# Differential attention mixed before the product, and the HGRN output norm moved to GpSimd

## The chip, the cores and the metric

One core of one Trainium2 chip runs the whole program. The metric is the device time of one launch in microseconds; 0.3% of it is 7.1 us.

## The reference, cut to what matters

The program is two transformer blocks on 512 tokens of width 1024, in float32. The change touches the mixer of the first layer only. Its two halves are a differential attention (4 heads, two score matrices of head width 64 each, values of width 128) and an HGRN2 recurrence (4 heads of width 128), both normed by an RMS norm over the 128 channels of a head:

```
s  = einsum('bhcqd,bhckd->bhcqk', q, k)          # c = 0, 1; causal mask
pr = softmax(s, axis=-1)
a  = pr[:, :, 0] - lam * pr[:, :, 1]
o_a = rms_norm(einsum('bhqk,bhkd->bhqd', a, v), sub_g) * (1 - lam_init)
o_b = rms_norm(hgrn_output, hg_g) * gate          # gate * hg_g is HG in the kernel
mix = concat([o_a, o_b]) @ w_out
```

## The kernel before, in words

Each engine has its own instruction list, written out by hand; they meet at counted semaphores. All large products run as three float32r products (high times high, high times low, low times high): ScalarE casts each 128x1024 weight piece to `w_h` (L803), VectorE makes the remainder `w_l` (L1300), TensorE multiplies (L2202).

The differential attention is a loop over 16 steps (4 heads, and in each head 4 tiles of 128 queries, with 128, 256, 384 and 512 keys, so each head is a period of 4 steps), called `diff_steps`. In its loop every engine handles several steps at once. At loop index k:

- TensorE: scores of step k for both c (`scores`, L2283), after VectorE's maxima of step k-2; transposes of both probability matrices of step k-2 (`trans`, L2292); products with the values of step k-3, one for each c (`values`, L2307). At k = 3 `keep_busy` (L2276) multiplies a weight piece 16 times into a bank that nobody reads. A float32 product is two instructions in the trace, a transpose is one.
- ScalarE: copies the transposed probabilities of step k-2 out of two PSUM banks in one instruction (`copy_pt`, L850), then the two exponentials of step k with their row sums (L841).
- VectorE: masks and takes the maxima of step k (`row_max`, L1436, in place for both c), then finishes step k-3 (`output` and `difference`): reciprocals of the row sums (L1446), times minus lambda (L1504), the two products scaled and added out of PSUM (L1505, L1506), and the square sum for the norm (L1495).
- GpSimd only issues DMAs; its next one (L716) waits for the last step's output.

The HGRN norm is laid between: its root (L907) is taken on ScalarE before the loop, VectorE forms the reciprocal at k = 1 (L1796) and scales `HI` at k = 2 to 5 (four 128x128 instructions of L1801 each). TensorE transposes the four 128-channel chunks of `HI` at k = 8, 10, 12 and 14 (L2455), ScalarE copies them at k = 9, 11, 13 and 15, after the exponentials of that step (L1100), and VectorE takes the remainder behind it at the same k (L1807).

After the loop `tail` begins: TensorE waits for the last output of the attention, multiplies two pieces of the output matrix with the HGRN half (L2202), then transposes the normed attention heads (L2244). Beside it ScalarE takes the root of the attention's norm (L907) and casts a piece, VectorE makes its remainder and norms 16 head tiles (L1818).

Of the kernel before, what the change touches and what calls it, by code (L numbers as in the profile page):

```python
# [24 lines left out]
P = 128  # L25
# [175 lines left out]
def bass_two_blocks(nc, t, consts, route_consts, tokens, slot_y, out):  # L201
    ctx = ExitStack()
    with ctx:
# [406 lines left out]
        OT_LAG = 4  # L610
        T_BANK, V_BANK, O_BANK = 4, 6, 7

        def row(v):

            return v.rearrange("(o n) -> o n", o=1).partition_broadcast(P) if len(v.shape) == 1 else v
# [98 lines left out]
        def _(pool):  # L714
            def load(dst, src_ap, name, **kw):
                pool.dma_start(dst, src_ap, **kw).then_inc(sem(name), 16)  # L716
# [15 lines left out]
            def tail(layer, mixer):  # L732
# [9 lines left out]
                load(GAIN[1], row(t["ln2_b"][layer]), "gain_a")  # L742

# [47 lines left out]
        def _(act):  # L791
# [310 lines left out]
            attention("diff", diff_steps, d_probs, d_pt, extra=hgrn_chunk)  # L1102
            root("sub", sd[:, 16:32], ms[:, 16:32], 1.0 / P, eps1)
# [182 lines left out]
        def _(dve):  # L1286
# [216 lines left out]
            def difference(k, w, inv):  # L1503
                own.mark(V.tensor_tensor(inv[:, 1:2], inv[:, 1:2], nlam, ALU.mult))  # L1504
                own.do(V.tensor_scalar(w.out, bank[V_BANK][:, 0:P], inv[:, 0:1], None, ALU.mult))  # L1505
                V.scalar_tensor_tensor(w.out, bank[V_BANK][:, P:2 * P], inv[:, 1:2], w.out, ALU.mult, ALU.add)\  # L1506
                    .then_inc(sem("at_out"), 1)
                dve.wait_ge(sem("at_out"), un.start["diff"] + k + 1)
                square_sum(w.out, 16 + 4 * (k % NT) + k // NT)
# [283 lines left out]
            def hgrn_norm(k):  # L1793
                if k == 1:
                    dve.wait_ge(sem("hg.root"), 1)
                    own.do(V.reciprocal(rs[:, 0:16], sd[:, 0:16]))  # L1796
                if 2 <= k < 6:
                    i = k - 2
                    for h in range(4):
                        hv = slice(h * P, (h + 1) * P)  # L1800
                        ins = V.scalar_tensor_tensor(HI[:, i, hv], HI[:, i, hv], rs[:, 4 * i + h:4 * i + h + 1],  # L1801
                                                     HG[:, i, hv], ALU.mult, ALU.mult)
                    ins.then_inc(sem("src_ready"), 1)
# [6 lines left out]
            attention("diff", diff_steps, d_probs, difference, extra=hgrn_norm)  # L1810
            tell(sem("sub.stat"))
# [347 lines left out]
        def _(pe):  # L2159
# [298 lines left out]
            attention("diff", diff_steps, d_probs, d_pt, warm=tail0[0][0], extra=hgrn_transposed)  # L2458
# [214 lines left out]
```

## Time and profile before

| | |
|---|---|
| median of 3 runs | 2375.17 us (2369.21 to 2375.31) |
| the profiled execution | 2371.46 us, its span 2369.6 us |
| TensorE busy, of the span | 94% |
| VectorE, ScalarE, GpSimd busy | 55%, 47%, 2% |
| the differential attention loop | about 210 to 265 us of the span |
| TensorE's granted clock, mean | 0.979 |

The span is that of the one core. Busy times of TensorE overlap a little, since its matmuls are pipelined; starts are exact, so distances between starts are what to read.

### The profile page before, as it was taken

How to read it: one execution, taken by the hardware profiler on the slowest of the kernel's cores; microseconds unless marked ns; L12 is line 12 of the kernel's file. 1: busy time of each engine (PE TensorE's matmuls, PEld its weight loads, DVE VectorE, ACT ScalarE, POOL GpSimd, SP SyncE). 2: the span in 40 equal slices, each digit the busy share in tenths (PEclk: the TensorE clock that was granted, in tenths of full speed). 3: DMA queues.
4: the chain of work that ended last, by engine and by line, in shares of the span. 5: the costliest groups of instructions: out<-in, count | busy, mean ns of one | idle time of the engine just before them, and what ended most of it. 6: DMA issues, size and time to landing. Idle time of an engine off the chain costs nothing.

```text
span 2369.6 us, 30065 instructions
## 1 busy us (share of the span) xinstructions
PE 2230.6 (94%) x11002; PEld 1819.0 (77%) x11002; DVE 1302.7 (55%) x1916; ACT 1107.1 (47%) x1646; POOL 54.8 (2%) x70
## 2 busy tenths in 40 slices
PE   6999999999999999999999999799999769999994
PEld 5877788888888776788888877568888558888883
DVE  3456663333374436553333467542454469998995
ACT  3435453433432237262442353363234358888884
POOL 1000000000000000000000000000000010000001
PEclk8999999999999999999999999899999979999997
DMA  5221233223322220233323232203223189999995
GB/s 166 94 71 36 74 105 103 93 96 98 98 89 89 80 72 1 89 125 98 97 91 104 80 107 93 63 28 97 90 72 98 58 332 403 410 410 408 409 401 186
DMA packets 129138, 338.59 MB, mean 143 GB/s; under 512 B 10528, under 2 KB 11712, under 8 KB 129040
## 3 DMA queue, kind: packets, MB, share of 16 engines
q1 hardware_dynamic: 117744, 296.85, 35.5%
q0 software_dynamic: 7840, 27.59, 3.4%
q10 hardware_dynamic: 3456, 12.81, 1.3%
q8 instruction: 65, 1.06, 0.2%
q14 instruction: 33, 0.27, 0.0%
HBM read 320.96 MB, written 16.25 MB: 142 GB/s over the span
## 4 chain that ended last, share of the span: by engine, by line
PE 86%; DVE 8%; ACT 4%; DMA 1%; issue 1%; SPq 0%; POOL 0%; DVEq 0%; ACTq 0%; POOLq 0%
PE bank L2202 40%; PE bank L2205 18%; PE bank L2582 10%; PE bank L2619 5%; PE bank L2283 2%; PE bank L2292 2%; PE bank L2353 1%; PE bank L2226 1%; DVE w_l L1300 1%; PE bank L2562 1%; PE bank L2307 1%; DMA w_raw<-in_ev_w_in_dram 1%; ACT w_h L803 1%; DVE stat L1332 1%; DVE xt_l L1367 1%
## 5 line engine op out<-in xcount | busy, mean ns | idle before, releaser
L1300 DVE TENSOR_TENSOR w_l<-w_raw,w_h 128x1024 fp32r<-128x1024 f32 x370 | 447.8, 1222 | 615.2 <-ACT w_h L803 612.1
L803 ACT CAST w_h<-w_raw 128x1024 fp32r<-128x1024 f32 x370 | 385.6, 1051 | 748.3 <-PE bank L2202 521.6
L2202 PE MATMUL bank<-w_h,xt_h 128*128 128x512 f32 (+1 forms) x960 | 377.2, 393 | 18.2 <-DVE w_l L1300 7.5
L2202 PE MATMUL bank<-w_h,xt_l 128*128 128x512 f32 (+1 forms) x960 | 372.5, 388 | 0.0
L2202 PE MATMUL bank<-w_l,xt_h 128*128 128x512 f32 (+1 forms) x960 | 372.4, 388 | 0.0
L2205 PE MATMUL bank<-xt_h,w_h 128*128 128x512 f32 x608 | 237.5, 391 | 12.0 <-DVE xt_l L1322 9.6
L2202 PE MATMUL bank<-w_h,ht_h 128*128 128x512 f32 x624 | 244.0, 391 | 0.7 <-DVE w_l L1300 0.7
L1300 DVE TENSOR_TENSOR w_l<-spare,w_h 128x1024 fp32r<-128x1024 f32 x184 | 220.6, 1220 | 41.5 <-ACT w_h L803 41.1
L2202 PE MATMUL bank<-w_h,ht_l 128*128 128x512 f32 x624 | 242.9, 389 | 0.0
L2202 PE MATMUL bank<-w_l,ht_h 128*128 128x512 f32 x624 | 242.8, 389 | 0.0
L2205 PE MATMUL bank<-xt_h,w_l 128*128 128x512 f32 x608 | 237.3, 390 | 0.0
L2205 PE MATMUL bank<-xt_l,w_h 128*128 128x512 f32 x608 | 237.1, 390 | 0.0
L2202 PEld LDWEIGHTS bank<-w_h,xt_h 128*128 128x128 f32 x960 | 181.4, 189 | 58.4 <-issue 12.0
L803 ACT CAST w_h<-spare 128x1024 fp32r<-128x1024 f32 x184 | 193.7, 1053 | 49.9 <-PE bank L2619 22.9
L2202 PEld LDWEIGHTS bank<-w_h,xt_l 128*128 128x128 f32 x960 | 181.5, 189 | 37.3
L2202 PEld LDWEIGHTS bank<-w_l,xt_h 128*128 128x128 f32 x960 | 181.7, 189 | 35.1
L2582 PE MATMUL bank<-w_h,xt_h 128*128 128x512 f32 x368 | 148.9, 405 | 2.4 <-DVE xt_l L2104 2.4
L2582 PE MATMUL bank<-w_h,xt_l 128*128 128x512 f32 x368 | 145.0, 394 | 0.0
L2582 PE MATMUL bank<-w_l,xt_h 128*128 128x512 f32 x368 | 144.1, 391 | 0.0
L2205 PEld LDWEIGHTS bank<-xt_h,w_h 128*128 128x128 f32 x608 | 114.6, 188 | 36.8 <-issue 13.0
L2202 PEld LDWEIGHTS bank<-w_h,ht_h 128*128 128x128 f32 x624 | 117.1, 188 | 25.5 <-DVE w_l L1300 1.5
L2202 PEld LDWEIGHTS bank<-w_h,ht_l 128*128 128x128 f32 x624 | 117.1, 188 | 24.3
(355 smaller groups left out, 2926.3 us busy)
## 6 DMA issues: line engine op xcount, KB each, us to landing
w_raw<-in_ffn_w_dram SPq DMA_DIRECT2D x128, 512.0 KB, 3.7
spare<-in_w_down_dram SPq DMA_DIRECT2D x92, 512.0 KB, 6.9
spare<-in_w_gate_dram SPq DMA_DIRECT2D x88, 512.0 KB, 7.2
w_raw<-in_w_up_dram SPq DMA_DIRECT2D x88, 512.0 KB, 6.6
w_raw<-in_w_in_dram SPq DMA_DIRECT2D x30, 512.0 KB, 3.8
w_raw<-in_ev_w_in_dram SPq DMA_DIRECT2D x28, 512.0 KB, 3.6
w_raw<-in_od_w_in_dram SPq DMA_DIRECT2D x24, 512.0 KB, 3.7
slot_y_dram<-slot_out ACTq DMA_DIRECT2D x23, 512.0 KB, 6.8
```

The lines of the kernel that those rows point to most:

```text
L803: nc.scalar.copy(w_h[:, n % SLOTS, :], raw_of(n)).then_inc(sem("w_hi"), 1)
L1300: V.tensor_tensor(w_l[:, s_, :], raw_of(n), w_h[:, s_, :].bitcast(F32), ALU.subtract)\
L1332: own.mark(V.bn_stats(bn[:, i, a, :], src_v[:, i, a * HALF:(a + 1) * HALF]))
L1367: V.tensor_tensor(xt_l[:, chunks, toks_of(i)], tile_bank(name, i, half).rearrange("p (c s) -> p c s", c=4), xt_h[:, chunks, toks_of(i)].bi ...
L2202: mm = T.matmul(bank[set0 + m][:, 0:g.width], a[:, c, toks_of(m)], b[:, kk, :], start=first, stop=last)
L2205: mm = T.matmul(bank[set0 + m][:, 0:g.toks], b[:, kk, m * P:(m + 1) * P], a[:, c, 0:g.toks], start=first, stop=last)
L2226: mm = T.transpose(tile_bank(name, i, half)[:, toks_of(c)], src_tile(i, 4 * half + c), ident)
L2283: T.matmul(bank[2 * (k % 2) + c][:, 0:w.keys], q, key, start=True, stop=True)\
L2292: mm = T.transpose(bank[T_BANK + c][:, toks_of(b)], probs[:, k % 3, c, toks_of(b)], ident)
L2307: mm = T.matmul(bank[V_BANK][:, c * w.dv:(c + 1) * w.dv], pt[:, k % 2, c, toks_of(b)], v, start=b == 0, stop=b == len(w.values[c]) - 1)
L2582: mm = T.matmul(bank[g.bank[0]][:, :], a, b[:, kk, :], start=j == kk == p == 0, stop=j == 3 and kk == 1 and p == 2)
L2619: mm = T.matmul(bank[g.bank[half]][:, :], a[:, j, :], b, start=j == p == 0, stop=j == 3 and p == 2)
```

## The change

`OUTPUT` is 3. The two probability matrices of a step are scaled by their reciprocal sums (the second also by minus lambda) and added on VectorE right after the exponentials. One matrix per step is then transposed, copied and multiplied. The output of a step leaves PSUM by a plain copy on VectorE; its square sum moves to ScalarE. The scaling of the HGRN output moves to GpSimd, as 16 scalings of `HG` and 4 multiplications into `HI`, which start when VectorE has the reciprocals at k = 1. The transposes alternate between two PSUM banks. The new TensorE loop has no `keep_busy`. The attention's root now waits for ScalarE's own squares.

```diff
@@ GpSimd, before tail(0, "dilated")
+            pool.wait_ge(sem("hg.scale"), 1)
+            for i in range(NT):
+                for h in range(4):
+                    hv = slice(h * P, (h + 1) * P)
+                    nc.gpsimd.tensor_scalar(HG[:, i, hv], HG[:, i, hv], rs[:, 4 * i + h:4 * i + h + 1], None, ALU.mult)                        .then_inc(sem("hg.scaled"), 1)
+            for i in range(NT):
+                pool.wait_ge(sem("hg.scaled"), 4 * i + 4)
+                nc.gpsimd.tensor_tensor(HI[:, i, :], HI[:, i, :], HG[:, i, :], ALU.mult).then_inc(sem("src_ready"), 1)
@@ ScalarE
-            attention("diff", diff_steps, d_probs, d_pt, extra=hgrn_chunk)
-            root("sub", sd[:, 16:32], ms[:, 16:32], 1.0 / P, eps1)
+                for k in range(n + OUTPUT):
+                    if k >= OUTPUT:
+                        u = k - OUTPUT
+                        col = 16 + 4 * (u % NT) + u // NT
+                        act.wait_ge(sem("at_out"), u + 1)
+                        nc.scalar.activation(spare[...], diff_steps[u].out,
+                                             ACT.Square, accum_out=ms[:, col:col + 1]).then_inc(sem("at_square"), 1)
+                    if TRANS <= k < n + TRANS:
+                        t_, w = k - TRANS, diff_steps[k - TRANS]
+                        act.wait_ge(sem("at_trans"), t_ + 1)
+                        if t_ >= 2:
+                            act.wait_ge(sem("at_values"), t_ - 1)
+                        nc.scalar.copy(d_pt[:, t_ % 2, 0, 0:w.keys], bank[T_BANK + t_ % 2][:, 0:w.keys])\
+                            .then_inc(sem("at_ptcopy"), 1)
+                    if k < n:
+                        for c in range(2):
+                            p = d_probs[:, k % 3, c, 0:diff_steps[k].keys]
+                            act.wait_ge(sem("at_max"), 2 * k + c + 1)
+                            nc.scalar.activation(p, p, ACT.Exp, scale=-1.0, bias=neg_max[:, k % 4, c:c + 1],
+                                                 accum_out=row_sum[:, k % 4, c:c + 1]).then_inc(sem("at_prob"), 1)
+                    hgrn_chunk(k)
+            act.wait_ge(sem("at_square"), len(diff_steps))
+            nc.scalar.activation(sd[:, 16:32], ms[:, 16:32], ACT.Sqrt, bias=eps1, scale=1.0 / P)
@@ VectorE
+                for k in range(n + OUTPUT):
+                    if k < n:
+                        row_max(0, k, diff_steps[k], d_probs)
+                    if k >= OUTPUT:
+                        u = k - OUTPUT
+                        dve.wait_ge(sem("at_values"), u + 1)
+                        V.tensor_copy(diff_steps[u].out, bank[V_BANK][:, 0:P]).then_inc(sem("at_out"), 1)
+                    if 1 <= k <= n:
+                        c = k - 1
+                        p0, p1 = (d_probs[:, c % 3, b, 0:diff_steps[c].keys] for b in range(2))
+                        inv = inv_sum[:, c % 2, :]
+                        dve.wait_ge(sem("at_prob"), 2 * c + 2)
+                        own.do(V.reciprocal(inv, row_sum[:, c % 4, :]))
+                        own.do(V.tensor_scalar(p1, p1, inv[:, 1:2], nlam, ALU.mult, ALU.mult))
+                        V.scalar_tensor_tensor(p0, p0, inv[:, 0:1], p1, ALU.mult, ALU.add).then_inc(sem("at_mixed"), 1)
+                    hgrn_norm(k)
@@ TensorE
+                for k in range(n + OUTPUT):
+                    if k < n:
+                        scores(0, k, diff_steps[k])
+                    if k >= OUTPUT:
+                        u, w = k - OUTPUT, diff_steps[k - OUTPUT]
+                        pe.wait_ge(sem("at_ptcopy"), u + 1)
+                        if u:
+                            pe.wait_ge(sem("at_out"), u)
...
+                    if TRANS <= k < n + TRANS:
+                        t_ = k - TRANS
+                        pe.wait_ge(sem("at_mixed"), t_ + 1)
...
+                    hgrn_transposed(k)
```

## Rows read from the trace of the kernel before

**Rows 1.** The page's first part: busy time, share of the span, instructions.

```profile
PE 2230.6 (94%) x11002; PEld 1819.0 (77%) x11002; DVE 1302.7 (55%) x1916; ACT 1107.1 (47%) x1646; POOL 54.8 (2%) x70
```

**Rows 2.** Busy time in a stretch: from:to, length, engines, granted clock, DMA.

```profile
220.00:230.00 10.00, 9.80 (x69) 7.14 (x70) 9.60 (x46) 6.91 (x20) 0.00 (x0) 1.00 0.01 2
```

**Rows 3.** Chain of waits, in order of time: start, length, what.

```profile
215.25 3.85 PE bank L2276 x16
...
224.09 1.05 DVE arena L1801 x4
...
264.92 8.46 PE bank L2202 x36
273.38 1.43 PE bank L2244 x13
```

**Rows 4.** TensorE's timeline: start, length, line, count, idle before with its releaser.

```profile
210.05 2.00 PE L2283 MATMUL bank<-arena 64*128 64x128 f32 x12 [1.06 <-ACT arena L824]
...
247.01 1.09 PE L2292 MATMUL bank<-cst,arena 128*128 128x128 f32 x8
...
250.63 2.02 PE L2307 MATMUL bank<-spare,arena 128*128 128x128 f32 x16
```

**Rows 5.** VectorE's timeline.

```profile
210.57 0.29 DVE L1436 CUSTOM_DVE_ANT_0 arena<-bank,cst 128x128 f32<-128x128 f32 x1 [7.02 <-PE bank L2283]
...
215.39 0.69 DVE L1436 CUSTOM_DVE_ANT_0 arena<-bank,cst 128x512 f32<-128x512 f32 x1 [1.31 <-PE bank L2283]
...
216.62 0.08 DVE L1436 DVE_READ_ACCUMULATOR2_ANT small<- 128x1 f32 x1
...
229.01 0.16 DVE L1446 RECIPROCAL small<-small 128x2 f32<-128x2 f32 x1
...
230.26 0.69 DVE L1436 CUSTOM_DVE_ANT_0 arena<-bank,cst 128x512 f32<-128x512 f32 x1
...
250.74 0.69 DVE L1807 TENSOR_TENSOR xt_l<-bank,xt_h 128x512 fp32r<-128x512 f32 x1
...
267.99 4.29 DVE L1818 SCALAR_TENSOR_TENSOR arena<-arena,stat,small 128x128 f32<-128x128 f32 x16
```

**Rows 6.** ScalarE's timeline.

```profile
212.93 0.40 ACT L841 ACTIVATE arena<-arena,small 128x128 f32<-128x128 f32 x1
...
213.71 0.49 ACT L841 ACTIVATE arena<-arena,small 128x256 f32<-128x256 f32 x1
...
219.57 0.58 ACT L850 COPY arena<-bank 128x512 f32<-128x512 f32 x1 [3.32 <-PE bank L2292]
220.06 0.72 ACT L841 ACTIVATE arena<-arena,small 128x512 f32<-128x512 f32 x1
...
221.48 0.78 ACT L850 COPY arena<-bank 128x768 f32<-128x768 f32 x1
...
260.16 1.28 ACT L907 ACT_TABLE_LOAD   x1
```

**Rows 7.** VectorE's groups by line and shape: count, busy, mean ns, idle before.

```profile
L1516 DVE SCALAR_TENSOR_TENSOR arena<-X,bank 128x512 f32<-128x512 f32 x16 | 10.8, 685 | 9.5 <-PE bank L2202 9.5
L1505 DVE TENSOR_SCALAR arena<-bank,small 128x128 f32<-128x128 f32 x16 | 5.5, 344 | 0.0
L1687 DVE TENSOR_SCALAR arena<-arena,small 128x512 f32<-128x512 f32 x4 | 2.2, 544 | 0.1
```

**Rows 8.** GpSimd's only 128x512 computation, of its groups by line.

```profile
L718 POOL MEMSET arena<- 128x512 f32 x1 | 0.5, 524 | 0.3 <-POOLq L2653 0.3
```

**Rows 9.** Busy time around two loops' ends: the second ("dilated") and this one.

```profile
946.00:956.00 10.00, 6.22 (x65) 4.47 (x63) 5.01 (x11) 5.68 (x10) 1.20 (x2) 1.00 0.01 2
...
958.00:962.00 4.00, 4.00 (x14) 3.14 (x12) 0.00 (x0) 0.00 (x0) 0.00 (x0) 0.64 0.99 286
966.00:970.00 4.00, 4.00 (x20) 3.30 (x19) 0.07 (x1) 1.05 (x1) 0.00 (x0) 1.00 0.43 131
...
251.00:264.00 13.00, 10.81 (x81) 8.80 (x80) 8.28 (x35) 6.83 (x14) 0.00 (x0) 1.00 0.01 1
```

More of the change, by code:

```diff
@@ L610, in bass_two_blocks @@
         OT_LAG = 4
+        OUTPUT = 3
         T_BANK, V_BANK, O_BANK = 4, 6, 7
@@ L1501, in scaled, with differences @@
                                 inv.unsqueeze(2).to_broadcast([P, 2, w.dv]), ALU.mult).then_inc(sem("at_out"), 1)
[L1503 to L1509, printed above, removed]
+            def differences():
+                n = len(diff_steps)
+                for k in range(n + OUTPUT):
[14 more added lines that the diff above has]
+                    hgrn_norm(k)
             def tail(layer, groups):
@@ L1795, in hgrn_norm @@
                     dve.wait_ge(sem("hg.root"), 1)
[L1796 to L1803, printed above, removed]
+                    V.reciprocal(rs[:, 0:16], sd[:, 0:16]).then_inc(sem("hg.scale"), 1)
                 if k in (9, 11, 13, 15):
@@ L1808, in hgrn_norm @@
                         .then_inc(sem("tr_lo"), 1)
-            attention("diff", diff_steps, d_probs, difference, extra=hgrn_norm)
-            tell(sem("sub.stat"))
+            differences()
             split(tail0[0][0].n + LOOK, None, 0)
@@ L2456, in hgrn_transposed, with differences @@
                     mm.then_inc(sem("tr_done"), 1)
-            attention("diff", diff_steps, d_probs, d_pt, warm=tail0[0][0], extra=hgrn_transposed)
+            def differences():
+                n = len(diff_steps)
+                for k in range(n + OUTPUT):
[6 more added lines that the diff above has]
+                            pe.wait_ge(sem("at_out"), u)
+                        for b, v in enumerate(w.values[0]):
+                            mm = T.matmul(bank[V_BANK][:, 0:P], d_pt[:, u % 2, 0, toks_of(b)], v,
+                                          start=b == 0, stop=b == len(w.values[0]) - 1)
+                        mm.then_inc(sem("at_values"), 1)
+                    if TRANS <= k < n + TRANS:
+                        t_ = k - TRANS
+                        pe.wait_ge(sem("at_mixed"), t_ + 1)
+                        if t_ >= 2:
+                            pe.wait_ge(sem("at_ptcopy"), t_ - 1)
+                        for b in range(diff_steps[t_].keys // P):
+                            mm = T.transpose(bank[T_BANK + t_ % 2][:, toks_of(b)], d_probs[:, t_ % 3, 0, toks_of(b)],
+                                             ident)
+                        mm.then_inc(sem("at_trans"), 1)
+                    hgrn_transposed(k)
+                pe.wait_ge(sem("at_out"), n)
+            differences()
             tail(0, tail0)
```

6 lines of the change are left out of this document (added).

## The prediction

> **What bounds the kernel now.** TensorE is busy 94% of the span [rows 1], so only a stretch where it waits, or does work that can go, is worth anything. The change touches one such stretch, 210 to 265 us. In the stretch table TensorE (9.8 of 10 us) and VectorE (9.6) are both full [rows 2]; ScalarE is not. The chain of waits says what set the pace: the 16 idle multiplications of L2276 (3.85 us), then VectorE with the HGRN scalings (1.05 us for four, in four steps), later TensorE [rows 3]. The loop ends at 264.87, TensorE's product begins at 264.92 [rows 3]. All that the change can win is how much earlier that product begins; call the loop's end T. The whole loop lasts 54 us, so even 10% of it is 0.23% of the kernel.
>
> **TensorE, removed.** Of each step's transposes and value products half go. The 8 transposes of a 512-key step take 1.09 us, the 16 instructions of its products 2.02 [rows 4]; a head has 20 and 40 of these, so 2.7 and 5.0 us, and half is 3.9 us per head, 15 over four. L2276's 3.85 us go too. TensorE is left with about 3 us of scores, 1.4 of transposes, 2.5 of products, in two heads 0.9 for HGRN: some 7 to 8 us per head, where a head took 12. It is no longer the bound.
>
> **VectorE, removed and added.** The finish of a step took 229.01 to 230.26, 1.25 us [rows 5], 20 us in all, and the 16 HGRN scalings 4.3 [rows 3]; both go. Added are, per step, a 128x128 copy out of PSUM and the mixing. The copy: the nearest rows are a 0.29 us instruction that is followed 0.21 later by the next, and L1505 with 0.34 [rows 5, 7]; I take 0.21, as nothing waits for its end on VectorE. Mixing: a reciprocal, 0.19 with its wait [rows 5]; the scaling, whose nearest rows are 0.344 at 128 columns and 0.544 at 512 [rows 7], so 0.34, 0.41, 0.48, 0.54 plus 0.03 for the wait; the two-input instruction, 0.27 at 128 (1.05 for four of L1801 [rows 3]) and 0.65 at 512 (0.685 less the overlap [rows 7]). Sums for 128, 256, 384, 512 keys: 0.83, 1.03, 1.23, 1.41, so 4.5 per head. Bounds: the scaling at the two-input rate (0.69 at 512) adds 0.3 per head; at half its rate (0.27) it takes 0.5 off. The maxima stay: 2 x (0.29 - 0.08) = 0.43 at 128 keys, 1.22 at 512 [rows 5], 0.70 and 0.96 between, 3.3 per head. VectorE now has 3.3 + 0.85 + 4.5 = 8.65 us per head without HGRN work, and it is the bound.
>
> **The new waits.** ScalarE gets a square per step at the head of its loop index, waiting for VectorE's copy of step k-3, which stands behind the maxima of step k. So from the end of the maxima of step k ScalarE needs 0.34 (copy, signals), 0.39 (square, by the 0.39 pace of a 128-column exponential with its sum), the copy of one matrix (0.17 to 0.49 [rows 6]) and the exponentials of step k: 0.78 at 128 keys, 1.42 at 512 [rows 6], 0.98 and 1.22 between. VectorE meanwhile does copy, mixing of k-1 and the maxima of k+1, then needs those exponentials. Most steps fit; the mixing of a 512-key step comes 0.37 too early, and the product of step 3 delays k = 6 by 0.4. At k = 9 and 13 VectorE also waits for ScalarE's HGRN copy, queued behind the exponentials: 0.34 + 0.39 + 0.49 + 0.98 + 0.57 + 0.05 = 2.82, then its own 0.60 (0.69 less the overlap [rows 5]), so 3.42 after the maxima, where copy and mixing alone take 1.04. At k = 11 and 15: 0.34 + 0.39 + 0.25 + 1.42 + 0.57 + 0.05 + 0.60 = 3.62. Behind the waiting VectorE stand the next maxima, and all engines wait for these.
>
> **Sum, clock kept.** Maxima of step 0 at 210.57 as before. The first mixing needs the exponentials of step 0, done at 213.8 (212.93 plus two [rows 6]): mixed at 214.7, the HGRN reciprocal at 214.95, then 215.9 (maxima 2), 216.95, 218.15 and 218.35 (maxima 3, copy), 219.6 (mixing 2). k = 4: 0.43 + 0.21 + a wait for the exponentials of step 3 + 1.41, to 222.0; k = 5 1.75, k = 6 2.6, k = 7 2.66, to 229.0. k = 8 2.42, k = 9 4.12, k = 10 2.2, k = 11 4.84, to 242.6. k = 12 2.05 (no wait, ScalarE is ahead), k = 13 4.12, k = 14 2.2, k = 15 4.84, to 255.8. Then copy and mixing 15: 257.45; four transposes 0.65, copy 0.6, four products 1.13 with signals, copy 0.3: T = 260.4. Before it was 264.87: 4.5 us are won, of the 20 and more that TensorE lost in work. Of these, 6.7 us stand as VectorE's four waits for ScalarE (1.78, 1.58, 1.78, 1.58).
>
> **After T.** The root's table load (1.28 us) stood in the idle time before [rows 6]; now squares come last and it falls between the last square and the root. Square 0.5, load, root 0.3, cast and remainder of a piece 2.2, reciprocal 0.3, four scalings per tile: the four tiles are ready at T + 5.7 to T + 8.9, against T + 7.4 before (267.99 + 4.29 [rows 5]). TensorE reaches their transposes at T + 8.46 [rows 3] and the last tile's a microsecond later, so this costs nothing; without that cover of two pieces it would cost 1.5 us.
>
> **GpSimd.** It starts at about 215.0, and TensorE needs `HI` at k = 8, after the transposes of step 6, at about 229.3. So 20 instructions have 14.3 us, 0.71 each. The only row is a 128x512 memset of 0.524 [rows 8], where VectorE's two-input 128x512 takes 0.69 [rows 7]. Lower end, VectorE's speed: 16 x 0.35 + 4 x 0.69 = 8.4 us. Upper end, three times that: 25 us. I take something near 11, hidden. The Trainium skill, "GPSIMD Engine Reference", section "Engine selection", calls GpSimd about 2x slower on two inputs and about line rate on one: an estimate of 16 x 0.35 + 4 x 1.38 = 11 us, in time; no row here shows it. Its section "Key points" says that GpSimd shares SBUF interfaces with VectorE, which speaks against the change: both could be slowed from 215 to 226, where five mixings (5.5 us) stand.
>
> **The clock.** The other loop's end is the row to weigh: TensorE busy 6.2 of 10 us, then idle 2.3 us, and the granted clock fell (0.64 in 958 to 962, 14 matmuls in 4 us where 20 fit later [rows 9]); that is 6 x 0.2 = 1.2 us there and 1.6 with what lies ahead of it. This loop's end kept 1.00 with 10.8 of 13 [rows 9]. After the change TensorE does about 3.5 us of work in the last 9 (251 to 260), with a gap of over 2 us while the last mixing waits: I expect a fall to 1.2 GHz and charge 1.6. At the start TensorE is idle from 212.05 [rows 4] to 214.7 and does some 2.5 us of work up to 219.5, with no L2276 to fill it; a fall there is half hidden behind VectorE: 0.5. Together 2.1 us; bounds 0 and 5.
>
> **The forecast.** -4.5 + 2.1 = -2.4 us: 2371.5 becomes 2369.1 for an execution like the profiled one. That one stood 3.7 us below the median shown; against the median 2375.2 it is 2372.8.
>
> **Rivals.**
> 1. ScalarE's queue doesn't hold VectorE back at k = 9 to 15 (its squares or copies are shorter): the waits of 1.78, 1.58, 1.78, 1.58 go, 6.7 us, and with the clock's loss the change is -9, 2366. For: ScalarE has only about 8.3 us of work per head. Against: before, too, L1807 waited 0.43 us twice. 10%.
> 2. The clock stays at 1.00: -4.5, 2370.7. For: no fall here before. Against: rows 9. 20%.
> 3. The clock falls again and again, as TensorE has under 60% of work from k = 9 on: each fall costs up to 1.7 us, four of them 7; less 4.5, +2.5 to +5, 2379. Against: a slow TensorE is a busy one, 7.5 us of work become 14 per head. 12%.
> 4. Slower: GpSimd is late. At three times VectorE's times its 25 us end at 240; TensorE holds its k = 8 transposes, and with them scores 9, for 10 us, and all follow one for one: +8, 2383. It decides from 0.71 us mean per instruction, and turns the sign at about 0.85. The skill's shared interface would act here. 10%.
> 5. The forecast's own case, 2369 to 2375.5: 48%.
>
> **How the numbers follow.** What this measurement can tell is about 0.3%, 7 us. Faster than that needs rival 1 or a run of cheap terms: 0.12. Slower needs rival 4 or a bad 3: 0.16. The rest is 0.72. The range from 2365 to 2380 leaves out rival 4 and the far end of 1; unknown terms are mixing (-2 to +1.3), clock (0 to +5), and the median's own 4 us.
>
> **What would show it.** Right: the value products L2307 gone, their successors at half the count; L1807's instruction idle 1.5 to 1.8 us for ScalarE four times; VectorE's maxima of step 8 at about 229; TensorE's first product of the tail near 260.4; granted clock under 1 in the 4 us behind it; GpSimd done before 229. Wrong: TensorE waiting for GpSimd at step 8, a scaling at 0.3 us per 512 columns or over 0.7, or a product of the tail waiting for the normed heads.

## The result, and the profile after

The changed kernel takes 2375.7 us (median of 20 runs, 2373.5 to 2380.3) where the kernel before takes 2370.9 (20 runs beside it, 2367.3 to 2376.6): a ratio of 1.0017, 95% interval 1.0010 to 1.0025. By the ratio it is 4 us slower (the medians lie 4.8 apart), where 2.4 us of gain were forecast. The profiled execution has a span of 2371.8 us, before 2369.6.

The page's first part, which answers to [rows 1]: TensorE lost 6.8 us of busy time and 136 instructions, and the time did not follow. About 20 us less work was forecast for TensorE; a part of its remaining work ran at half the clock and so counts for more busy time.

```profile
PE 2223.8 (94%) x10866; PEld 1809.7 (76%) x10866; DVE 1304.0 (55%) x1868; ACT 1107.6 (47%) x1678; POOL 69.8 (3%) x90
```

The stretch table from the first scores to the first product of the tail (I call this the loop), and the 12 us behind it: first the kernel after, then the kernel before, whose loop ran from TensorE's 210.05 [rows 4] to 264.92 [rows 3].

```profile
208.60:268.23 59.63, 42.63 (x200) 27.83 (x200) 41.13 (x133) 33.83 (x118) 15.37 (x20) 0.76 0.00 1
268.23:280.23 12.00, 12.00 (x57) 10.12 (x58) 7.39 (x20) 5.17 (x9) 2.44 (x4) 0.92 0.74 236
```
```profile
210.05:264.92 54.87, 49.20 (x337) 36.96 (x337) 39.37 (x180) 34.80 (x88) 0.00 (x0) 1.00 0.00 1
264.92:276.92 12.00, 12.00 (x61) 10.19 (x62) 8.55 (x24) 4.35 (x7) 2.36 (x4) 1.00 0.77 257
```

The loop became 4.76 us longer, at a mean granted clock of 0.76 in place of 1.00, and the tail's first pieces lost 0.9 us more: from the first product to the heads' transposes TensorE took 9.19 us (to 277.42), before 8.30 (to 273.22; the 8.46 of [rows 3] is a busy time that overlaps them). The spans differ by less: this loop happened to start 1.45 us earlier, and behind the other loop the clock fell before (0.64 [rows 9]) and not after (1.00 in all of 956 to 970), which is 1.6 us by the prediction's reckoning. The loops of the kernels below start anywhere from 208.13 to 211.62 us, though nothing ahead of them was changed, so I compare loops and ratios, not spans.

VectorE's timeline around step 5's mixing, then GpSimd's. The columns are start, length, what, and in brackets the idle time before with its releaser.

```profile
214.50 0.45 DVE L1555 TENSOR_SCALAR arena<-arena,small 128x256 f32<-128x256 f32 x1
...
217.51 0.62 DVE L1556 SCALAR_TENSOR_TENSOR arena<-arena,small 128x384 f32<-128x384 f32 x1
...
225.16 3.94 DVE L1555 TENSOR_SCALAR arena<-arena,small 128x256 f32<-128x256 f32 x1
229.15 0.48 DVE L1556 SCALAR_TENSOR_TENSOR arena<-arena,small 128x256 f32<-128x256 f32 x1
229.55 0.68 DVE L1472 CUSTOM_DVE_ANT_0 arena<-bank,cst 128x512 f32<-128x512 f32 x1
```
```profile
213.59 10.46 POOL L749 TENSOR_SCALAR arena<-arena,stat 128x128 f32<-128x128 f32 x16 [206.68 <-DVE stat L1844]
224.03 4.93 POOL L752 TENSOR_TENSOR arena<-arena 128x512 f32<-128x512 f32 x4
```

A scaling of 128x256 that takes 0.45 us at 214.50 takes 3.94 at 225.16. It ends at 229.10, 0.14 after the last of GpSimd's four two-input products (224.03 + 4.93 = 228.96). During GpSimd's 16 scalings, which have one tensor input, VectorE ran at its usual pace.

TensorE's timeline:

```profile
217.63 1.22 PE L2509 MATMUL bank<-spare,arena 128*128 128x128 f32 x4 [0.70 <-ACT arena L1126]
...
229.68 0.69 PE L2518 MATMUL bank<-cst,arena 128*128 128x128 f32 x2 [3.37 <-DVE arena L1556]
231.80 1.22 PE L2509 MATMUL bank<-spare,arena 128*128 128x128 f32 x4 [0.70 <-ACT arena L1126]
...
244.50 0.71 PE L2509 MATMUL bank<-spare,arena 128*128 128x128 f32 x4 [1.26 <-ACT arena L1126]
...
262.60 1.65 PE L2509 MATMUL bank<-spare,arena 128*128 128x128 f32 x6 [2.46 <-ACT arena L1126]
...
265.78 2.07 PE L2509 MATMUL bank<-spare,arena 128*128 128x128 f32 x8 [0.67 <-ACT arena L1126]
268.23 0.80 PE L2242 MATMUL bank<-w_h,xt_h 128*128 128x512 f32 x1 [0.39 <-DVE arena L1548]
```

At 229.68 it had waited 3.37 us for the mixed matrix behind that scaling. The same four instructions take 1.22 us at one place and 0.71 at another: the clock. The stretch table in pieces of 4 us (the clock is the third number from the end; 0.50 is 1.2 GHz, 1.00 is 2.4) shows four falls, the last of them in the drain, by which I mean the steps after the last scores:

```profile
216.00:220.00 4.00, 3.30 (x14) 2.47 (x15) 3.51 (x16) 2.86 (x11) 4.00 (x7) 0.50 0.00 0
...
224.00:228.00 4.00, 2.31 (x14) 1.20 (x12) 3.96 (x7) 2.22 (x9) 4.00 (x5) 1.00 0.00 0
...
232.00:236.00 4.00, 4.00 (x17) 3.02 (x18) 2.57 (x10) 2.73 (x11) 0.00 (x0) 0.50 0.03 6
...
240.00:244.00 4.00, 3.03 (x16) 1.52 (x16) 3.89 (x16) 1.97 (x8) 0.00 (x0) 1.00 0.00 0
...
248.00:252.00 4.00, 4.00 (x18) 2.86 (x18) 2.79 (x10) 1.81 (x10) 0.00 (x0) 0.50 0.00 0
...
264.00:268.00 4.00, 3.17 (x14) 2.48 (x12) 0.41 (x2) 0.99 (x3) 0.00 (x0) 0.50 0.00 0
```

VectorE's four waits for ScalarE's HGRN copy, and its last copy:

```profile
239.45 0.69 DVE L1848 TENSOR_TENSOR xt_l<-bank,xt_h 128x512 fp32r<-128x512 f32 x1 [1.55 <-ACT xt_h L1110]
...
246.37 0.69 DVE L1848 TENSOR_TENSOR xt_l<-bank,xt_h 128x512 fp32r<-128x512 f32 x1 [1.37 <-ACT xt_h L1110]
...
253.94 0.69 DVE L1848 TENSOR_TENSOR xt_l<-bank,xt_h 128x512 fp32r<-128x512 f32 x1 [1.79 <-ACT xt_h L1110]
...
260.86 0.69 DVE L1848 TENSOR_TENSOR xt_l<-bank,xt_h 128x512 fp32r<-128x512 f32 x1 [1.37 <-ACT xt_h L1110]
...
267.89 0.29 DVE L1548 COPY arena<-bank 128x128 f32<-128x128 f32 x1 [3.31 <-PE bank L2509]
```

### The profile page after: what moved, and what is told of

Read it like the earlier page. It is cut to its first block, busy times and chain, and to the rows that moved or that the text cites. A ratio compares the mean times of both kernels' runs of the same rounds, so it can differ in the third digit from the quotient of the medians.

```text
span 2371.8 us, 29784 instructions
## 1 busy us (share of the span) xinstructions
PE 2223.8 (94%) x10866; PEld 1809.7 (76%) x10866; DVE 1304.0 (55%) x1868; ACT 1107.6 (47%) x1678; POOL 69.8 (3%) x90
## 3 DMA queue, kind: packets, MB, share of 16 engines
q8 instruction: 63, 1.03, 0.2%
## 4 chain that ended last, share of the span: by engine, by line
PE 85%; DVE 8%; ACT 4%; issue 1%; DMA 1%; POOL 0%; SPq 0%; ACTq 0%; DVEq 0%; POOLq 0%
PE bank L2242 40%; PE bank L2245 18%; PE bank L2648 10%; PE bank L2685 5%; PE bank L2323 2%; PE bank L2332 2%; PE bank L2393 1%; DVE w_l L1336 1%; PE bank L2266 1%; PE bank L2628 1%; ACT w_h L813 1%; DMA X<-in_x_dram 1%; DVE stat L1368 1%; DVE xt_l L1403 1%; ACT arena L834 1%
```

## The experiments

The theories: A, GpSimd's norm blocks VectorE; B, the clock falls because TensorE has too little to do; C, ScalarE's order (the square ahead of a step's exponentials, HGRN's copy behind them) holds VectorE. The recorded expectations call them Theory 2, Theory 1 and Theory 3; those of d1_chunk and d2_square use the letters A to C for other things. All ran beside the kernel before. "Loop" is as above, from each one's profiled execution; the kernel before has 54.87 us at clock 1.00, the changed one 59.63 at 0.76. There is one trace of each kernel, and it need not be a typical execution: that of a7_pieces is the shortest of five (2374.7, median 2378.8), that of a5_order the longest of seven (2368.8, median 2365.5), that of d2_square 3.3 us under its median.

| kernel | loop, us | clock | median / beside it before, us | ratio [95%] |
|---|---|---|---|---|
| a1_keep | 60.71 | 0.82 | 2376.4 / 2373.9 | 1.0025 [1.0010, 1.0040] |
| a2_norm | 57.06 | 0.78 | 2374.3 / 2373.9 | 1.0007 [0.9997, 1.0017] |
| a3_both | 59.27 | 0.85 | 2377.5 / 2373.9 | 1.0017 [1.0007, 1.0027] |
| b1_pool | 62.51 | 0.92 | 2376.9 / 2373.9 | 1.0013 [1.0004, 1.0021] |
| a7_pieces | 58.26 | 0.77 | 2378.8 / 2370.8 | 1.0035 [1.0022, 1.0049] |
| c4_one_input | 56.05 | 0.77 | 2374.5 / 2372.8 | 1.0012 [1.0002, 1.0022] |
| a4_fill | 56.19 | 0.97 | 2373.2 / 2370.8 | 1.0003 [0.9994, 1.0012] |
| a5_order | 51.30 | 0.97 | 2365.5 / 2370.8 | 0.9976 [0.9965, 0.9987] |
| a6_order | 51.09 | 0.80 | 2366.3 / 2370.8 | 0.9976 [0.9966, 0.9985] |
| c3_before_order | 56.02 | 0.97 | 2372.3 / 2372.8 | 0.9992 [0.9982, 1.0003] |
| d1_chunk | 51.35 | 0.84 | 2368.9 / 2372.0 | 0.9992 [0.9980, 1.0003] |
| d2_square | 54.49 | 0.78 | 2374.3 / 2372.0 | 1.0004 [0.9992, 1.0016] |
| c1_order_pool | 50.12 | 0.80 | 2366.4 / 2372.8 | 0.9975 [0.9966, 0.9985] |
| c2_split | 49.53 | 0.83 | 2365.7 / 2372.8 | 0.9979 [0.9970, 0.9989] |
| d3_split_fill | 46.93 | 0.96 | 2363.0 / 2372.0 | 0.9962 [0.9948, 0.9976] |

### Idle products back, and the norm back on VectorE

a1_keep, from the changed kernel, after the scores of k = 3:

```diff
+                    if k == 3:
+                        keep_busy(tail0[0][0], 16, O_BANK)
```

> The changed kernel with the 16 idle multiplications put back at k = 3. Theory 1 (the granted clock): in the changed kernel it fell to 1.2 GHz at 215.5, 229, 246.5 and 260; the filling ends the first fall only. It takes 3.9 us itself at full clock, most of it in front of VectorE's next maxima, so the loop stays at 59 to 61 us (59.6 without) and the kernel within 1.5 us of the changed one. Rival (the missing idle multiplications are what made the change lose): the clock stays at 1.00 through the loop, the loop gets 3 us or more shorter. Theory 2 (GpSimd blocks VectorE): the 3.9 us scaling of 256 columns stays in either case.

a2_norm, from the changed kernel (GpSimd's 20 instructions gone):

```diff
-                    V.reciprocal(rs[:, 0:16], sd[:, 0:16]).then_inc(sem("hg.scale"), 1)
+                    own.do(V.reciprocal(rs[:, 0:16], sd[:, 0:16]))
+                if 2 <= k < 6:
+                    i = k - 2
+                    for h in range(4):
+                        hv = slice(h * P, (h + 1) * P)
+                        ins = V.scalar_tensor_tensor(HI[:, i, hv], HI[:, i, hv], rs[:, 4 * i + h:4 * i + h + 1],
+                                                     HG[:, i, hv], ALU.mult, ALU.mult)
+                    ins.then_inc(sem("src_ready"), 1)
```

> The changed kernel with the HGRN norm back on VectorE (16 scalings at k = 2 to 5). Theory 2 (GpSimd's four two-input instructions, 224.0 to 229.0, hold a port that VectorE's scaling of probabilities needs): no such scaling takes over 0.6 us where one took 3.94; the 3.5 us are won, the scalings cost up to 4.3, and the clock's fall at 229 goes or moves: loop 57.5 to 60 us against 59.6, the kernel 0 to 2 us faster. Rival (the 3.94 us come from ScalarE or from TensorE and only show there): a scaling of 3 us or more stays, and the kernel is 4 us slower.

a3_both has both edits.

> Both at once: the norm on VectorE and the 16 idle multiplications at k = 3. Under theories 1 and 2 together no first fall of the clock, no blocked scaling; loop 58 to 61 us, since the HGRN scalings of VectorE fall beside the idle multiplications as before the change, and the kernel at the time of the one before (within 3 us). Rival (neither matters, it is ScalarE's queue alone): the loop stays at 59.6 plus what was put back, 62 or more.

TensorE of a1_keep, and VectorE's mixing of step 3 with the block in another place:

```profile
218.20 5.82 PE L2316 MATMUL bank<-w_h 128*128 128x512 f32 x16
```
```profile
224.28 0.29 DVE L1548 COPY arena<-bank 128x128 f32<-128x128 f32 x1 [4.55 <-PE bank L2511]
...
226.91 1.54 DVE L1555 TENSOR_SCALAR arena<-arena,small 128x512 f32<-128x512 f32 x1
228.49 1.63 DVE L1556 SCALAR_TENSOR_TENSOR arena<-arena,small 128x512 f32<-128x512 f32 x1
```

The idle products stand in front of work: the copy of step 0 waited 4.55 us behind them, and the loop grew by 1.1 us. They did not prevent the first fall either: the granted clock was 0.50 from 216 to 222, and the 16 took 5.82 us where they took 3.85 before [rows 3]. Of a1_keep's twelve executions seven took 2373.6 to 2376.9 us and five 2382.6 to 2386.1; the trace is of one of the seven, and what made the five longer is open.

The norm on VectorE takes 2.6 us off the loop though VectorE has 4.3 us more to do [rows 3]. That speaks for A, and 2.2 us over the kernel before stay. In the times it is not clear of the noise: 1.0007 [0.9997, 1.0017] against 1.0017 [1.0010, 1.0025]. Both edits together (a3_both) have a loop of 59.27, as expected, but did not come within 3 us of the kernel before: the idle products cost 2.2 us of loop over a2_norm, most of what the norm's move gave.

### The norm on GpSimd alone

b1_pool is the kernel before with only the GpSimd part: its 20 instructions in, VectorE's 16 out.

> The kernel before with only the HGRN norm moved to GpSimd. It has no VectorE instruction in this loop that reads and writes SBUF alone with one input, so under theory 2 nothing is blocked: VectorE loses 4.3 us of scalings in k = 2 to 5, on the path there, and the loop gets 1.5 to 4 us shorter (54.9 before); the kernel 1.5 to 4 us faster. Rival (GpSimd slows all of VectorE's SBUF work, or is late at k = 8): the maxima of 224 to 229 take longer than 0.7 us, or TensorE waits for GpSimd, and nothing is won.

VectorE, GpSimd and TensorE of b1_pool:

```profile
221.72 4.50 DVE L1514 TENSOR_TENSOR small<-small 128x1 f32<-128x1 f32 x1
...
229.29 0.16 DVE L1514 TENSOR_TENSOR small<-small 128x1 f32<-128x1 f32 x1
```
```profile
221.26 4.93 POOL L752 TENSOR_TENSOR arena<-arena 128x512 f32<-128x512 f32 x4
```
```profile
227.01 2.04 PE L2310 MATMUL bank<-spare,arena 128*128 128x128 f32 x8 [4.30 <-DVE arena L1516]
```

A multiplication of one element per partition, which takes 0.16 us elsewhere, took 4.50 and ended at 226.22 with GpSimd's products (226.19). The expectation of no block fell: a two-input instruction of VectorE is held as well, here one of 128x1. This half of the change, by itself, makes the loop 7.6 us longer in the profiled execution and costs 1.3 per mille of the time, 3 us. Not all of the 7.6 is the block. An early fall of the clock stands ahead of it, and c3_before_order (below), which has nothing on GpSimd, has it too; first b1_pool, then c3_before_order:

```profile
214.00:218.00 4.00, 4.00 (x11) 2.05 (x11) 1.31 (x4) 2.17 (x9) 4.00 (x8) 0.57 0.00 0
```
```profile
216.00:218.00 2.00, 2.00 (x5) 1.04 (x4) 1.02 (x3) 0.94 (x4) 0.00 (x0) 0.50 0.00 0
```

Counted from the first scores, VectorE's maxima of step 4 come 1.6 us later than in the kernel before in c3_before_order, and 5.9 us later in b1_pool: 1.6 of early fall and 4.3 of block. Another 1.6 us follow up to step 9, where the clock is down again (0.54 in 224 to 230). How often an execution has such a block and how long it is, one trace can't say.

### What of GpSimd's work blocks

a7_pieces cuts each of GpSimd's products into four:

```diff
-                nc.gpsimd.tensor_tensor(HI[:, i, :], HI[:, i, :], HG[:, i, :], ALU.mult).then_inc(sem("src_ready"), 1)
+                for h in range(4):
+                    hv = slice(h * P, (h + 1) * P)
+                    ins = nc.gpsimd.tensor_tensor(HI[:, i, hv], HI[:, i, hv], HG[:, i, hv], ALU.mult)
+                    ins.then_inc(sem("hg.product"), 1)
+            for i in range(NT):
+                pool.wait_ge(sem("hg.product"), 4 * i + 4)
+                pool.sem_inc(sem("src_ready"), 1)
```

> The changed kernel with GpSimd's four two-input multiplications of 128x512 cut into 16 of 128x128. Theory 2a (VectorE gets the port only between GpSimd's two-input instructions, and only when GpSimd lets go): with pieces of about 0.4 us VectorE's scaling waits at most 0.5 us at a time and its longest takes under 1.5 us, the loop 56 to 58 us. Theory 2b (a run of queued two-input instructions holds the port to its end): the scaling again takes 3 to 6 us, to the end of the last piece, and the loop is 59.6 or more.

c4_one_input gives them one tensor input; what it leaves out is the product of the HGRN output with its gate:

```diff
-                nc.gpsimd.tensor_tensor(HI[:, i, :], HI[:, i, :], HG[:, i, :], ALU.mult).then_inc(sem("src_ready"), 1)
+                nc.gpsimd.tensor_scalar(HI[:, i, :], HI[:, i, :], 1.0, None, ALU.mult).then_inc(sem("src_ready"), 1)
```

> The changed kernel with GpSimd's four 128x512 products of two inputs replaced by four 128x512 scalings by 1.0 of one input; what it leaves out is the product of the HGRN output with its gate. If two inputs are what takes the port: no VectorE scaling above 0.7 us, loop 55 to 57 us against 59.6. Rival (any GpSimd instruction of 512 columns holds the port): a VectorE instruction of 1.5 us or more stays in 224 to 229, the loop 58 to 60.

GpSimd of a7_pieces and VectorE's scaling of step 5 in it, then the same two of c4_one_input:

```profile
225.10 7.50 POOL L754 TENSOR_TENSOR arena<-arena 128x128 f32<-128x128 f32 x16
```
```profile
226.62 0.75 DVE L1561 TENSOR_SCALAR arena<-arena,small 128x256 f32<-128x256 f32 x1
```
```profile
225.71 5.98 POOL L752 TENSOR_SCALAR arena<-arena 128x512 f32<-128x512 f32 x4
```
```profile
226.66 0.68 DVE L1555 TENSOR_SCALAR arena<-arena,small 128x256 f32<-128x256 f32 x1
```

With one input GpSimd is busy longer (1.50 us per 128x512, where two inputs took 1.23), and VectorE loses at most 0.3 us on an instruction in place of 3.5, about 1 us over four instructions. The loop is 3.6 us shorter than with two inputs. So A is shown in the traces: what holds VectorE for long is GpSimd's 128x512 products of two tensor inputs, not its being busy. The price in time is not pinned: 1.0012 [1.0002, 1.0022] with one input, 1.0017 [1.0010, 1.0025] with two. In pieces of 128x128 the long block is gone too, with two inputs; but only 1.4 us of the loop are, and 0.7 of those are lost again behind it (9.92 us to the heads' transposes, 9.19 in the changed kernel). GpSimd's products last 7.50 us in place of 4.93. Its ratio, 1.0035, is the worst of all, which its trace, of the shortest of its five executions, does not explain; that stays open.

### The clock

a4_fill is a2_norm with idle 128x512 products (`filler`) ahead of TensorE's wait for each mixed matrix, 61 in all, and a wait for the weight piece that they read ahead of the loop (not shown):

```diff
-                        pe.wait_ge(sem("at_mixed"), t_ + 1)
                         if t_ >= 2:
                             pe.wait_ge(sem("at_ptcopy"), t_ - 1)
+                        filler(10 if t_ == 0 else 6 if k >= n else 3, T_BANK + t_ % 2)
+                        pe.wait_ge(sem("at_mixed"), t_ + 1)
```

> The changed kernel with the HGRN norm on VectorE and idle 128x512 multiplications before each wait for a mixed matrix: 10 at the first, 3 at each step, 6 at the last two. With the norm on VectorE alone the loop took 57.06 us and the granted clock was 0.78 in it. Theory 1 (the falls of the clock cost the time): the clock stays at 0.97 or more, TensorE's transposes and products take half, and the loop comes to 52 to 54.5 us; the product behind it runs at full clock, another 0.8 us. The kernel is 3 to 6 us faster than the changed one with the norm on VectorE. Rival (the clock is only a sign of idle time; VectorE and ScalarE set the pace): the clock stays up and the loop stays at 56 to 58, as the idle products stand in front of each transpose.

The clock came back to 0.97, the loop only by 0.9 us. B alone falls as the explanation: with the clock up, 56.19 us is still longer than the 54.87 of before. But 0.9 us is what the clock gives back less what the idle products cost: at the end of the loop six of them (1.63 us) stand ahead of the last transposes, and VectorE's last copy waits as long as in the changed kernel (3.37 and 3.31 us).

### ScalarE's order

a5_order is a4_fill, a6_order is a2_norm, each with the same change of ScalarE's step (told in words, where the code has the instructions shown in "The change"):

```diff
                 for k in range(n + OUTPUT):
-                    square of step k - 3
                     copy of the transposed matrix of step k - 2
+                    hgrn_chunk(k)
                     the two exponentials of step k
-                    hgrn_chunk(k)
+                    square of step k - 3
```

> As the one with idle multiplications at each step, and ScalarE's order changed: the HGRN chunk before the exponentials, the square after them. Theory 3 (ScalarE's queue order holds VectorE: its waits for the HGRN copy are 1.55, 1.37, 1.79 and 1.37 us in the changed kernel, and the copy of the transposed matrix stands behind the square): the waits go, 5 to 7 us over the loop, and it takes 46 to 49 us, the kernel 5 us faster than the one before. Rival (VectorE's own work is full: 41 us busy): the waits only move, and the loop is 51 us or more.

> ScalarE's order changed as above and the norm on VectorE, but no idle multiplications. Theory 3 without theory 1: four waits of 1.4 to 1.8 us go and the clock still falls: loop 51 to 54 us against 57.06. Rival (the order matters only when TensorE is fast): with the clock down the loop stays over 55.

Both loops are 5 to 6 us shorter (56.19 to 51.30, 57.06 to 51.09), and both kernels beat the kernel before by 2.4 per mille. Here the filled pauses bring nothing. a5_order's 51.30 is over the 46 to 49 us expected: of VectorE's four waits for HGRN's copy two stay, at 1.03 and 0.70 us.

d1_chunk is a2_norm with only `hgrn_chunk(k)` moved, d2_square with only the square moved.

> Reference points: the changed kernel with HGRN's output norm back on VectorE and ScalarE's order as it was took 57.06 us from the first scores to the first product of the tail; with both parts of ScalarE's order turned round (HGRN's copy ahead of the two exponentials of a step, the square of a head's output behind them) it took 51.09. Here HGRN's copy alone is moved ahead; the square stays ahead of the exponentials and waits there for VectorE. Theory A (the copy, late by the order, is what held VectorE: its four waits of 1.4 to 1.8 us): the loop is 51 to 52.5 us and the time about 2366. Theory B (the square, which waits 25 us in all for VectorE with the exponentials behind it, is what held the loop): 55 to 57 us, time 2370 to 2373. Theory C (shared): between, 53 to 55.

> The other half of the order alone: the square of a head's output stands behind the step's exponentials, HGRN's copy stays at the end of ScalarE's step. Theory A (the late copy holds VectorE): the four waits of VectorE for the copy stay at 1.4 to 1.8 us and the loop is 55 to 57 us, time about 2371 to 2373. Theory B (the square holds it): 51 to 52.5 us and 2366. Theory C: 53 to 55 us. Sum of both gains should come to about the 6.0 us of both together if they don't cover each other.

The first two of VectorE's waits for HGRN's copy, in a2_norm, d1_chunk and d2_square:

```profile
239.76 0.69 DVE L1846 TENSOR_TENSOR xt_l<-bank,xt_h 128x512 fp32r<-128x512 f32 x1 [1.56 <-ACT xt_h L1101]
...
246.69 0.69 DVE L1846 TENSOR_TENSOR xt_l<-bank,xt_h 128x512 fp32r<-128x512 f32 x1 [1.38 <-ACT xt_h L1101]
```
```profile
236.25 0.69 DVE L1846 TENSOR_TENSOR xt_l<-bank,xt_h 128x512 fp32r<-128x512 f32 x1 [0.59 <-ACT xt_h L1101]
```
```profile
237.74 0.69 DVE L1846 TENSOR_TENSOR xt_l<-bank,xt_h 128x512 fp32r<-128x512 f32 x1 [1.58 <-ACT xt_h L1101]
...
243.74 0.69 DVE L1846 TENSOR_TENSOR xt_l<-bank,xt_h 128x512 fp32r<-128x512 f32 x1 [0.45 <-ACT xt_h L1101]
```

With the copy moved, two of the four waits are 0.59 us and the other two are gone; the loop gains 5.7 us of the 6.0 that both parts give. The square alone gains 2.6, partly since two of these waits fall to 0.45 (the other two are 1.58 and 2.09); its 54.49 us lie in the band that the expectation called C. The two gains add up to 8.3 us, so they overlap. In the loop the late copy is the larger part. In the times this is less clear: d2_square can't be told from a2_norm (1.0004 and 1.0007), and the ratio of d1_chunk (0.9992) lags behind a6_order's (0.9976) by more than its loop. From the first product of the tail to the heads' transposes 9.95 us pass in d1_chunk, at a clock of 0.82, and 8.31 at 1.00 in a6_order. That is 1.6 us more of the 3.8; the rest is open.

c3_before_order gives the kernel before the early HGRN copy:

```diff
+                    if extra:
+                        extra(k)
                     the two exponentials of step k
-                    if extra:
-                        extra(k)
```

> The kernel before with only ScalarE's HGRN chunk put before the exponentials. There VectorE waited 0.43 us twice for it, and TensorE is the bound: the loop is 54 to 55 us against 54.87, the kernel the same within 1 us. Rival (the order alone brings what the reordered kernels won, not the single mixed matrix): 52 us or less.

Nothing is won there in time, and the loop, 56.02 us, is over the 54 to 55 expected. The early fall of the clock shown under b1_pool accounts for that: 1.6 us are lost by step 4, and 0.5 won after it. The order pays only together with the mixing.

### The best arrangement

c1_order_pool is the changed kernel with a6_order's order: everything of the change kept.

> The changed kernel, HGRN norm still on GpSimd, with only ScalarE's order changed (HGRN chunk before the exponentials, square after them). With the norm on VectorE that order took the loop from 57.06 to 51.09 us. If the order's gain and the port's loss add (theory): loop 59.6 - 6 = 53 to 54.5 us, the kernel 2 to 4 us faster than the one before, with one VectorE instruction of 3 us or more still in it. Rival (VectorE, blocked by GpSimd, leaves nothing for the order to win): 57 or more.

c2_split has that order too, and lets GpSimd do only the 16 one-input scalings and VectorE the four products:

```diff
-            for i in range(NT):
-                pool.wait_ge(sem("hg.scaled"), 4 * i + 4)
-                nc.gpsimd.tensor_tensor(HI[:, i, :], HI[:, i, :], HG[:, i, :], ALU.mult).then_inc(sem("src_ready"), 1)
+                if 4 <= k < 8:
+                    i = k - 4
+                    dve.wait_ge(sem("hg.scaled"), 4 * i + 4)
+                    V.tensor_tensor(HI[:, i, :], HI[:, i, :], HG[:, i, :], ALU.mult).then_inc(sem("src_ready"), 1)
```

> As above, but GpSimd makes only the 16 one-input scalings and VectorE the four 128x512 multiplications at k = 4 to 7 (0.62 us of its time each). Port theory: no VectorE instruction above 0.8 us, VectorE has 1.8 us less than with the whole norm (4.3), and the loop is 48.5 to 50.5 us against 51.09; the kernel 6 to 8 us faster than the one before. Rival (GpSimd's one-input work slows VectorE too): the mixings of 214 to 224 take 0.3 us or more longer each, and the loop is no shorter than 51.

d3_split_fill is c2_split with idle products where TensorE had pauses:

```diff
+                        if t_ in (0, 14):
+                            filler(8 if t_ == 0 else 5, T_BANK + t_ % 2)
                         pe.wait_ge(sem("at_mixed"), t_ + 1)
```

> The fastest arrangement so far (GpSimd only scales, VectorE forms the four products, ScalarE's order turned round; loop 49.53 us at a mean granted clock of 0.83) with 8 idle 128x512 products on TensorE ahead of its wait for the first mixed matrix and 5 ahead of that of step 14, so that it has no pause there. Theory 1 (the clock still costs 1 to 2 us in the loop and some 0.8 behind it): granted clock above 0.93, loop 48 to 49 us, time 1 to 2.5 us below the same kernel without them. Theory 2 (the idle products stand in front of work and give back nothing): loop 49.3 to 50.5, time within 1 us of it, even with a higher clock.

VectorE of c1_order_pool, still partly blocked, in its two instructions that lost most, then the loop in the stretch table of c2_split and of d3_split_fill:

```profile
224.68 1.37 DVE L1556 SCALAR_TENSOR_TENSOR arena<-arena,small 128x256 f32<-128x256 f32 x1
...
227.58 1.05 DVE L1555 TENSOR_SCALAR arena<-arena,small 128x384 f32<-128x384 f32 x1
```
```profile
210.52:260.05 49.53, 39.90 (x201) 25.60 (x201) 39.48 (x137) 33.66 (x118) 11.05 (x16) 0.83 0.00 1
```
```profile
211.36:258.29 46.93, 37.75 (x214) 24.05 (x214) 39.27 (x137) 33.63 (x118) 11.17 (x16) 0.96 0.00 1
```

c1_order_pool's loop, 50.12 us, is shorter than the 53 to 54.5 expected, and no VectorE instruction of 3 us is in it: GpSimd's products are the same, and VectorE lost 0.9 and 0.6 us beside them in place of 3.5. So the block is not always as long as in the changed kernel's trace. c1, c2 and a6 can't be told apart by their times: with ScalarE's order turned round, it makes no difference that can be measured here whether the norm is on GpSimd or on VectorE. (Behind the loop c1's trace takes 10.19 us to the heads' transposes, those of c2 and a6 8.29 and 8.31.) The 13 idle products of d3 take 2.6 us off the loop of c2, more than was expected of them; in the times the two kernels' intervals just overlap. Filling two real pauses pays, where filling every step (a4_fill, a5_order) gave 0.9 us and nothing. Against the kernel before, d3 is faster by 3.8 per mille (2.4 to 5.2), 9 us; against the changed kernel it is about 13.

## Why the prediction was wrong

**The steps that failed** are two: the GpSimd term, which enters the sum at nothing ("I take something near 11, hidden"), and the sum of the loop itself, which holds that TensorE "is no longer the bound" and gives VectorE no more than 0.4 us of waiting for it. Set the maxima of the changed kernel against the dates of the sum, both counted from the first scores (208.60 and 210.05):

| | lateness, us | grows by |
|---|---|---|
| maxima of step 4 | -0.1 | |
| step 6 | 1.5 | 1.6 |
| step 7 | 4.65 | 3.2 |
| step 9 | 5.9 | 1.2 |
| step 12 | 5.8 | 0 |
| step 14 | 7.2 | 1.4 |
| end of the loop | 9.3 | 2.1 |

**GpSimd: 3.2 us, between steps 6 and 7.** Its start was as summed (213.59, which is 215.0 less the 1.45 us of the earlier loop). It lasted 15.4 us, over the 14.3 that the summed pace allowed, and was done at 228.96; but TensorE came to `HI`'s first transposes at 233.46, since the loop was late itself, and in c1_order_pool, where it came at 230.04, it did not wait for them either. What was missing is what GpSimd's products do to VectorE, the engine that sets the pace. The prediction named this ("both could be slowed from 215 to 226") and gave it no price. It was placed wrongly as well: nothing happened in the 10.5 us of scalings, all of it in the 4.9 us of products. Measured: 3.5 us on one instruction of the changed kernel, 3.6 us of the loop (c4_one_input), 1.5 us over two instructions in c1_order_pool. With 3.6 us the forecast of -2.4 becomes +1.2, no longer a gain; it does not by itself make the 4 us.

What would have warned of it is the Trainium skill's "SBUF — State Buffer", section "Who interferes with whom" ("only the shared port pair causes contention, and it's an exclusive lock"): a VectorE instruction with two SBUF inputs and a GpSimd instruction that reads SBUF, or a VectorE instruction in a two-port mode and any GpSimd instruction, hold each other off for a whole instruction. This case agrees that an instruction can be held outright (0.16 us became 4.50), and differs twice: the block outlasted single instructions of GpSimd (3.94 us beside products of 1.23), and one-input instructions, which read SBUF too, cost VectorE 0.0 to 0.3 us. In which mode VectorE's scalings ran, no trace here shows.

**TensorE and its clock: the other 6.1 us.** The prediction charged "together 2.1 us" for two falls. There were four, which is rival 3's picture, and every growth outside GpSimd's block stands at one of them or right behind it. VectorE waited for TensorE 0.34, 0.16, 0.70 and 0.39 us by the maxima of step 6, 0.34, 1.02 and 0.17 from 233 to 237, 0.40 and 0.70 from 249 to 251; where the clock was 1.00, from 238 to 246 and from 254 to 259, it waited for it nowhere. Two of these:

```profile
222.27 0.29 DVE L1548 COPY arena<-bank 128x128 f32<-128x128 f32 x1 [0.70 <-PE bank L2509]
...
235.81 0.42 DVE L1472 CUSTOM_DVE_ANT_0 arena<-bank,cst 128x256 f32<-128x256 f32 x1 [1.02 <-PE bank L2323]
```

In the drain the last four transposes took 1.06 us and the last eight products 2.07, where 0.60 and 1.16 stand elsewhere in the same loop, and the transposes stood 0.85 us behind the products of the step before, which the sum had left out. (Its last addition, 257.45 + 0.65 + 0.6 + 1.13 + 0.3, also gives 260.1 and not 260.4.) Against rival 3 the prediction held "a slow TensorE is a busy one"; it is, but VectorE then waits for it. Behind the loop the clock cost 0.9 us more.

How much of the 6.1 us is the clock alone is not measured, since no kernel here is the changed one with its clock kept. By filling the pauses 0.9 us came back (a4_fill, which has 61 idle products and the 4.3 us of the norm on VectorE) or 2.6 (d3_split_fill, in the better order). The rest goes with the order: TensorE's products of a step wait for ScalarE's copy, which stands behind the square, which waits for VectorE's copy, which waits for TensorE's products of the step before (0.70 us at 217.63 and 231.80 above), a ring whose members the sum had added one by one. This is argued from dates. Turning the order round, which takes the square out of the ring, made c1_order_pool's loop 9.5 us shorter than the changed kernel's at a clock of 0.80, some 2 us of it by the shorter block.

**What was right.** VectorE's four waits for the late HGRN copy: predicted 1.78, 1.58, 1.78, 1.58, measured 1.55, 1.37, 1.79, 1.37. So were the lengths of the mixing (0.35, 0.45, 0.48 and 0.55 for the scalings where nothing blocks), and the dates of the first steps: the maxima of step 4 as summed, those of step 5 0.2 us late. The table load fell where it was put, at 268.63, between the last square and the root, and nothing waited for the normed heads: VectorE was done with them at 276.92, TensorE's transposes began at 277.42. Rival 4's mechanism, a late GpSimd, did not happen; its sign did, by the sharing that the prediction laid beside it. That GpSimd was not late was partly luck: its end, 228.96, is 1.1 us behind the summed date of `HI`'s transposes (229.3 less 1.45), and the loop's own lateness covered that.

Rival 1 is of interest though the changed kernel didn't go that way: "ScalarE's queue doesn't hold VectorE back ... 2366". Changing the order made it so, and the changed kernel with it (c1_order_pool) runs at 2366.4. That the number is rival 1's is chance: it stands 6 us under the kernel before beside it, not 9. The 6.7 us that the prediction had charged as fixed were the cheapest cost of the change to remove.

## What to carry to other kernels

Before moving work to GpSimd, look at what the busiest VectorE instructions read: long two-input products on GpSimd held VectorE's instructions with SBUF operands here, so try GpSimd with one-input work, or place its products beside VectorE's reads of PSUM, and measure, since the price changed with the timing. When a change empties one engine, ask what its clock will do and whether it is still in the ring that sets the pace. When a sum charges a wait because of the order inside an engine's step, try the order before the change: here it was worth 6 us of loop or more, the whole difference between slower and faster. Idle products paid where they filled a pause (d3_split_fill); in front of work they cost what they gave (a1_keep, a4_fill).

## What the runs showed of the hardware

- A queued run of GpSimd products of two SBUF inputs held one VectorE instruction until the run ended: 3.94 us for 0.45, 4.50 us for a 0.16 us instruction of 128x1. In other kernels' traces VectorE got in between two of them (1.54 and 1.63 us in a1_keep, 1.37 and 1.05 in c1_order_pool). No instruction of VectorE that reads PSUM was seen slowed beside them.
- GpSimd's times: 0.65 us per 128x128 scaling by a per-partition scalar, 0.47 per 128x128 two-input product, 1.23 per 128x512 two-input product, and 1.50 for a 128x512 one-input scaling: the one-input form was the slower.
- The granted clock fell to 1.2 GHz four times in a loop where TensorE was busy 42.6 of 59.6 us, and stayed at 2.4 GHz in the one of the kernel before, where it was busy 49.2 of 54.9; c3_before_order, whose TensorE has that same work, had one short fall (0.50 in 216 to 218).
